# First layer of a two-layer trunk step on one core: eight mixing units multiplied from the unnormalised input

## What is computed

```python
def _rms(x, g):
    xf = x.astype(jnp.float32)
    y = xf * lax.rsqrt(jnp.mean(xf * xf, axis=-1, keepdims=True) + EPS)
    return (y * g.astype(jnp.float32)).astype(x.dtype)

def _layer(x, cond, p, lam_init, pos, ctx):
    mod = jnp.einsum('bd,de->be', jax.nn.silu(cond), p['w_ada']) + p['b_ada']
    sh1, sc1, g1, sh2, sc2, g2 = jnp.split(mod[:, None, :], 6, axis=-1)
    h = _rms(x, p['g_norm1']) * (1 + sc1) + sh1
    u = h @ p['w_in']
    gates, xa, qkv_da, xc, mla_in = jnp.split(u, IN_SPLITS, axis=-1)
    ...
```

## Time and profile before

| | |
|---|---|
| median of 3 runs | 1224.08 us (1223.28 to 1226.67) |
| the profiled execution, its time | 1223.51 us |
| its span | 1221.7 us |
| PE busy | 1208.0 us (99%) |
| DVE busy | 901.4 us (74%) |
| ACT busy | 575.6 us (47%) |
| POOL busy | 136.8 us (11%) |

### The profile page before, as it was taken

The page is one execution under the profiler, slowest core; times in us unless marked ns, Lnnn a source line. Parts: engine busy times, 40 slices in busy tenths (PEclk is TensorE's granted clock), DMA queues, the critical chain, the costliest instruction groups (busy, mean ns, idle before and its releaser), DMA issues.

```text
span 1221.7 us, 19781 instructions
## 1 busy us (share of the span) xinstructions
PE 1208.0 (99%) x7816; PEld 1149.7 (94%) x7816; DVE 901.4 (74%) x1671; ACT 575.6 (47%) x949; POOL 136.8 (11%) x109
## 2 busy tenths in 40 slices
PE   8999999999999999999999999999999999999998
PEld 7987999989989999999989889999998999999998
DVE  5597877748689999986876965765686887887432
ACT  3445564643365544532354455645425554454321
POOL 0232000008300000000202500000271000000000
PEclk9999999999999999999999999999999999999999
DMA  9763433444744444469664522332345334334443
GB/s 370 291 220 125 147 117 112 172 139 161 253 173 144 167 156 159 169 216 322 214 234 163 189 87 87 104 104 87 104 167 196 122 124 135 122 123 136 134 142 121
DMA packets 53532, 198.82 MB, mean 163 GB/s; under 512 B 6784, under 2 KB 7200, under 8 KB 51904
## 3 DMA queue, kind: packets, MB, share of 16 engines
q1 hardware_dynamic: 53120, 196.86, 46.0%
q0 software_dynamic: 320, 0.69, 0.2%
HBM read 195.25 MB, written 2.27 MB: 162 GB/s over the span
## 4 chain that ended last, share of the span: by engine, by line
PE 93%; DVE 2%; POOL 2%; DMA 1%; issue 1%; ACT 0%; SPq 0%; DVEq 0%; POOLq 0%; ACTq 0%
PE bank L1444 27%; PE bank L1446 27%; PE bank L1445 26%; PE bank L1743 1%; PE bank L1723 1%; PE bank L1512 1%; DVE w_lo L980 1%; DMA start_ada<-start_ada 1%; PE bank L1517 1%; PE bank L1516 1%; POOL wide L653 1%; PE bank L1713 1%; POOL merge_sum L655 1%; PE bank L1501 1%; PE bank L1698 1%
## 5 line engine op out<-in xcount | busy, mean ns | idle before, releaser
L1444 PE MATMUL bank<-act_hi,w_hi 128*128 128x384 f32 x1368 | 465.0, 340 | 0.7 <-DVE act_lo L1055 0.3
L1446 PE MATMUL bank<-act_hi,w_lo 128*128 128x384 f32 x1368 | 457.8, 335 | 0.0
L1445 PE MATMUL bank<-act_lo,w_hi 128*128 128x384 f32 x1336 | 446.6, 334 | 0.0
L980 DVE TENSOR_TENSOR w_lo<-w_raw,w_hi 128x1024 fp32r<-128x1024 f32 x251 | 318.9, 1272 | 114.6 <-ACT w_hi L662 113.6
L662 ACT ACTIVATE w_hi<-w_raw 128x1024 fp32r<-128x1024 f32 x251 | 264.3, 1054 | 167.8 <-DMA w_raw<-stream 167.7
L1444 PEld LDWEIGHTS bank<-act_hi,w_hi 128*128 128x128 f32 x1368 | 257.1, 188 | 10.7 <-issue 6.5
L1446 PEld LDWEIGHTS bank<-act_hi,w_lo 128*128 128x128 f32 x1368 | 256.8, 188 | 0.0
L1445 PEld LDWEIGHTS bank<-act_lo,w_hi 128*128 128x128 f32 x1336 | 251.0, 188 | 0.6
L1446 PE MATMUL bank<-mlp_hi,w_lo 128*128 128x384 f32 x352 | 118.3, 336 | 0.0
L1444 PE MATMUL bank<-mlp_hi,w_hi 128*128 128x384 f32 x352 | 118.3, 336 | 0.0
L1445 PE MATMUL bank<-mlp_lo,w_hi 128*128 128x384 f32 x352 | 118.3, 336 | 0.0
(11 more groups left out here) (246 smaller groups left out, 1576.0 us busy)
## 6 DMA issues: line engine op xcount, KB each, us to landing
w_raw<-stream SPq DMA_DIRECT2D x251, 512.0 KB, 3.3
ada<-ada_rows SPq DMA_DIRECT2D x48, 512.0 KB, 4.4
start_ada<-start_ada SPq DMA_DIRECT2D x8, 1024.0 KB, 17.9
ada_norm<-ada_w SPq DMA_DIRECT2D x16, 512.0 KB, 5.8
ada<-ada_w SPq DMA_DIRECT2D x8, 512.0 KB, 5.5
start_raw<-start_w SPq DMA_DIRECT2D x8, 448.0 KB, 18.5
ada_head_a<-ada_w SPq DMA_DIRECT2D x5, 512.0 KB, 7.3
cond_spread_mix<-cond_rows SPq DMA_DIRECT2D x2, 1024.0 KB, 7.9
```

What stands on the lines that cost most here:

```text
L980: V.tensor_tensor(wlo[s][:, :], raw[s][:, :], whi[s][:, :].bitcast(F32), ALU.subtract).then_inc(lo_ready, 1)
L1444: T.matmul(out, wb[s][0][:, w, :], hi[k], start=first and k == 0, stop=False)
L1445: T.matmul(out, wb[s][0][:, w, :], lo[k], start=False, stop=False)
L1446: ins = T.matmul(out, wb[s][1][:, w, :], hi[k], start=False, stop=last and k == n - 1)
```

## The change

- PE multiplies eight units (START_UNITS = 8) with x times scale, which is not divided by the root of the square sum, and with two more columns, the shift itself (`start_width` = 386 columns). The high and low parts of these operands are `suhi` and `sulo`. Afterwards DVE (`start_rescale`) multiplies each bank by `rstd` and ACT (`start_add_shift`) adds the product of weights and shift.
- The normalised input (`ahi`, `alo`), needed from `values` on, is still made: ACT leaves x times scale in `late` (`gated_late`), POOL multiplies it by `rstd`, ACT and DVE split it (`normed_high`, `normed_low`), by the table START_NORMED in blocks 4 to 7.
- The square sums: ACT squares two blocks at a time, POOL adds the eight squares to one block, and PE sums the partitions with one matmul in block 3, between the high and the low products.
- x is loaded in four parts, each ahead of a block's weights; START_ADA is 3, WARM 6.
- In `MIX`, `xc0` and `xc1` now stand before `k0` and `k1`, in both layers.

```diff
-START_ADA = 6
-WARM = 11
+START_ADA = 3
+WARM = 6
+START_UNITS = SKIP + 1
+START_NORMED = {4: (0,), 5: (1, 2), 6: (3, 4), 7: (5, 6)}
...
-MIX = ["xa0", "xa1", "q0", "q1", "k0", "k1", "xc0", "xc1", "v0", "v1", "cq", "ckv", "cqr"]
+MIX = ["xa0", "xa1", "q0", "q1", "xc0", "xc1", "k0", "k1", "v0", "v1", "cq", "ckv", "cqr"]
...
# SP
-            for h in range(2):
-                c0, c1 = h * KD // 2 * TOK, (h + 1) * KD // 2 * TOK
-                sp.dma_start(x_t[:, c0:c1], x_in[:, c0:c1]).then_inc(x_loaded[h], 16)
             for j in range(KD):
+                if j < KD // 2:
+                    c0, c1 = 2 * j * TOK, (2 * j + 2) * TOK
+                    sp.dma_start(x_t[:, c0:c1], x_in[:, c0:c1]).then_inc(x_loaded[j], 16)
                 if j >= START_ADA:
                     sp.wait_ge(ada_done, 2 * (j - START_ADA + 1))
...
# POOL
+                if l == 0:
+                    for h in range(KD // 2):
+                        pool.wait_ge(start_sq, h + 1)
+                        own(nc.gpsimd.tensor_tensor(wide[:, 2 * h, :], wide[:, 2 * h, :], wide[:, 2 * h + 1, :], ALU.add))
+                        own.wait()
+                        if h >= 1:
+                            own(nc.gpsimd.tensor_tensor(wide[:, 0, :], wide[:, 0, :], wide[:, 2 * h, :], ALU.add))
+                            own.wait()
+                    nc.gpsimd.sem_inc(start_sq_sum, 1)
+                    pool.wait_ge(rstd_ready, 1)
+                    for k in range(KD):
+                        pool.wait_ge(start_full, k + 1)
+                        nc.gpsimd.tensor_tensor(wide[:, k, :], late[:, k, :], rsn, ALU.mult).then_inc(norm_full, 1)
...
# ACT
+                def start_unnormed_high(j):
+                    act.wait_ge(start_shift, j + 1)
+                    for a, e, c in RANGES:
+                        ins = A(late[:, j, a:e], x[:, j, a:e], ACT.Copy, scale=sc1[:, j, c:c + 1])
+                    ins.then_inc(start_full, 1)
+                    A(suhi[:, j, TOK:start_width], mod[:, j, :], ACT.Copy)
+                    act.wait_ge(start_full, j + 1)
+                    A(suhi[:, j, 0:TOK], late[:, j, :], ACT.Copy).then_inc(start_u_hi, 1)
+                def start_add_shift(q):
+                    out = pj[:, PJ[MIX[q]], :]
+                    act.wait_ge(start_rescaled, q + 1)
+                    for a, e, c in RANGES:
+                        ins = A(out[:, a:e], out[:, a:e], ACT.Identity, bias=start_sums[:, q, c:c + 1])
+                    ins.then_inc(mix_out, 1)
                 if l == 0:
+                    for j in range(KD):
+                        if j < KD // 2:
+                            start_square(j)
+                        start_high(j)
+                        if j == KD // 2:
+                            roots(0)
+                        start_unnormed_high(j)
+                        for k in START_NORMED.get(j, ()):
+                            normed_high(0, k)
+                    split(SKIP)
+                    normed_high(0, KD - 1)
+                    split(SKIP + 1)
+                    for q in range(START_UNITS):
+                        start_add_shift(q)
+                        if q == 2:
+                            split(SKIP + 2)
+                        if MIX[q] in SQUARED:
+                            mix_squares(q)
...
# DVE
+                    start_low(j)
+                    dve.wait_ge(start_u_hi, j + 1)
+                    low(sulo[:, j, 0:TOK], late[:, j, :], suhi[:, j, 0:TOK])
+                    low(sulo[:, j, TOK:start_width], mod[:, j, :], suhi[:, j, TOK:start_width]).then_inc(start_u_lo, 1)
+                def start_rescale(q):
                     dve.wait_ge(rstd_ready, 1)
+                    dve.wait_ge(unit_done, FROM + q + 1)
+                    V.tensor_copy(start_sums[:, q, :], bank[q][:, TOK:start_width])
+                    V.tensor_tensor(pj[:, PJ[MIX[q]], :], bank[q][:, 0:TOK], rsn, ALU.mult).then_inc(start_rescaled, 1)
...
# PE
+                    pe.wait_ge(start_read, KD // 2 + 1)
+                    pe.wait_ge(start_sq_sum, 1)
+                    T.matmul(bank[7][:, P:P + TOK], cc("ones"), wide[:, 0, :], start=True, stop=True).then_inc(ss_done, 1)
...
                     pe.wait_ge(cond_ready, 1)
                     start_modulate(0)
-                    start_modulate(1)
                     for j in range(KD):
-                        start_products(j)
-                        if j + 2 < KD:
-                            start_modulate(j + 2)
+                        if 1 <= j < KD - 1:
+                            start_modulate(j + 1)
+                        start_high_products(j)
+                        if j == 0:
+                            start_modulate(1)
+                        if j == KD // 2 - 1:
+                            start_squares()
+                        start_low_products(j)
+                    unit_ready(SKIP)
+                    pe.wait_ge(mod_read, FROM + 2)
+                    dense(bank[7][:, 0:start_width], SKIP, range(KD), [suhi[:, k, :] for k in range(KD)],
+                          [sulo[:, k, :] for k in range(KD)]).then_inc(unit_done, 1)
```

More of the change, by code:

```diff
@@ L679, in square @@
                 A(wide[:, k:k + n, :], x[:, k:k + n, :], ACT.Square).then_inc(sq_ready, 1)
-            for h in range(2):
-                act.wait_ge(x_loaded[h], 16)
-                A(wide[:, 4 * h:4 * h + 2, :], x[:, 4 * h:4 * h + 2, :], ACT.Square).then_inc(start_sq_act, 1)
             own = Links(act, act_own)
@@ L708, in rstds, with roots, normed_high, norm @@
                             after[i]()
[L710 to L712 removed]
+                def roots(n):
                     act.wait_ge(ss_done, l * 2 + n + 1)
[L714 removed]
+                    sums = bank[SUM_BANK[n]][:, 0:TOK] if l + n else bank[7][:, P:P + TOK]
+                    own(A(rsn, sums, ACT.Ln, scale=1.0 / D, bias=EPSC))
                     own.wait()
                     A(rsn, rsn, ACT.Exp, scale=-0.5).then_inc(rstd_ready, 1)
[L717 removed]
+                def normed_high(n, k):
+                    shift = mod[:, 0:8, :] if n == 0 else mod[:, 24:32, :]
+                    act.wait_ge(norm_full, (l * 2 + n) * KD + k + 1)
+                    for a, e, c in RANGES:
+                        ins = A(ahi[:, k, a:e], wide[:, k, a:e], ACT.Identity, bias=shift[:, k, c:c + 1])
+                    ins.then_inc(norm_hi, 1)
+                def norm(n):
+                    roots(n)
+                    if n == 0:
                         act.wait_ge(shift_ready, l)
                     for k in range(KD):
[L720 to L726 removed]
+                        normed_high(n, k)
+                def mix_squares(u):
+                    i, rows = SQUARED.index(MIX[u]), NOPE if MIX[u] == "cqr" else P
+                    act.wait_ge(mix_out, l * U_MIX + u + 1)
+                    A(wide[0:rows, i, :], pj[0:rows, PJ[MIX[u]], :], ACT.Square).then_inc(psq, 1)
                 def start_high(j):
@@ L756, in _ @@
                     if name in SQUARED:
-                        i, rows = SQUARED.index(name), NOPE if name == "cqr" else P
-                        act.wait_ge(mix_out, l * U_MIX + u + 1)
-                        A(wide[0:rows, i, :], pj[0:rows, PJ[name], :], ACT.Square).then_inc(psq, 1)
+                        mix_squares(u)
                 def gate(g):
@@ L1038, in scales, with normed_low @@
                                                pc(gain).unsqueeze(2).to_broadcast([P, KD, 2]), ALU.add, ALU.mult))
+                def normed_low(n, k):
+                    shift = mod[:, 24 * n:24 * n + KD, :]
+                    dve.wait_ge(norm_hi, (l * 2 + n) * KD + k + 1)
+                    if l + n == 0:
+                        dve.wait_ge(start_u_lo, k + 1)
+                    for a, b, c in RANGES:
+                        ins = V.scalar_tensor_tensor(alo[:, k, a:b], wide[:, k, a:b], shift[:, k, c:c + 1],
+                                                     ahi[:, k, a:b].bitcast(F32), ALU.add, ALU.subtract)
+                    ins.then_inc(norm_lo, 1)
                 def norm(n):
-                    scale, shift = (sc1, mod[:, 0:8, :]) if n == 0 else (sc2, mod[:, 24:32, :])
+                    scale = (sc1, sc2)[n]
                     own.wait()
@@ L1098, in _ @@
                     for j in range(KD):
-                        start_norm(j)
-                    for u in range(SKIP, SKIP + 3):
-                        split(u)
+                        start_unnormed_low(j)
+                        for k in START_NORMED.get(j, ()):
+                            normed_low(0, k)
+                    split(SKIP)
+                    normed_low(0, KD - 1)
+                    split(SKIP + 1)
+                    for q in range(START_UNITS):
+                        start_rescale(q)
+                        if q == 2:
+                            split(SKIP + 2)
                 else:
@@ L1551, in values @@
                                 ins.then_inc(unit_done, 1)
```

(2 more changed lines are left out.)

126 lines of the change are left out of this document (52 added, 74 removed).

## The result

The changed kernel takes 1235.56 us (median of 4 runs, 1235.47 to 1237.72), the kernel before 1224.15 beside it: ratio 1.0099, interval 1.0085 to 1.0113. It is 11.4 us slower, where 3.35 were forecast, and outside the range of 1221.5 to 1229.5. The span grows by 12.0, from 1221.7 to 1233.7 us.

What follows compares the result with a forecast made beforehand. PE was taken as never idle from 19.77 us on, the start-up before it as bound by bytes. Terms -0.5 + 0.75 + 1.9 + 1.2 = +3.35 on 1223.51 gave 1226.8 us, range 1221.5 to 1229.5.

Steps and rivals of the forecast that it cites:

- Behind 100 us I see nothing: Rest of the kernel after 100 us: nothing gained or lost there; layer 1's new order only moves the same work.
- Term 3: Queue on ACT and DVE ahead of `values`: it starts 1.8 us after unit 7 ends; +1.9 in all, bounds 0 and 3.
- Term 1: Start of the kernel: fewer bytes of x ahead, modulation 2 at 19.25 instead of 19.77 us, -0.5 us.
- Term 2: Square sums: one f32 matmul comes back in block 3, on a PE without idle time, +0.75 us.
- blocks 4 to 7: Moved operations on ACT and DVE fit under each block's 4.87 us, costed at nothing; cover about 1 us per block.
- late bound: Start-up: PE's clock becomes high only at 17.9 us, which would make the start +0.45 us instead of -0.5.
- two extra columns: Unnormalised products: 2 columns in 384 over 192 matmuls of 0.17 us, 0.2 us, taken as inside the rounding.
- rival D: POOL stretches DVE's low parts in blocks 4 and 5; PE waits some 2.5 us, 1229.3 us; chance 0.23.
- Term 4: Row products on DVE start 4.6 us later, PE waits ahead of the products with `cq`: +1.2 us, bounds 0 and 3.3.
- B: Start: the clock is high early and bytes bound the start, -0.95 there, 1226.4 us in all; chance 0.18.
- C: Start: loads land earlier, clock high, modulation 2 at 16.8, -3.0 there; 1224.4 us, or 1221.3 without both waits; chance 0.17.

Runs made afterwards that it cites:

- filled_wait: Changed kernel with 13 small matmuls of `ones` by `ones` in PE's wait ahead of `values`: 1233.04 us, ratio 1.0079.
- shifts_first: both_fixes, with ACT doing the eight shifts in one go, then unit 10's high part, then the four squares: 1226.61 us, ratio 1.0024.
- warm_start: Changed kernel with 11 pairs of warm-up matmuls instead of 6 and 10 more matmuls behind modulation 0: 1234.07 us, ratio 1.008.
- no_shift_of_tiles: Changed kernel with its 64-byte tile `start_sums_shift` behind `start_unnormed_lo` instead of ahead of `mlp_hi`: 1231.01 us, ratio 1.0056.
- pool_held: Changed kernel with POOL's window operations held until DVE has made unit 9's low part: 1233.46 us, ratio 1.008.
- unit9_first: Changed kernel with unit 9's high part ahead of ACT's eight shifts and its low part behind DVE's first rescaling: 1231.3 us, ratio 1.0057.
- both_fixes: Changed kernel with the edits of unit9_first and no_shift_of_tiles together: 1227.4 us, ratio 1.0027.
- all_fixes: shifts_first with 11 pairs of warm-up matmuls and 10 more matmuls behind modulation 0: 1226.53 us, ratio 1.0025.
- mlp_tiles_64_on_before: Kernel before with `mlp_hi` and the tiles laid behind it 64 bytes further on, no instruction changed: 1226.76 us, ratio 1.002.
- x_behind: all_fixes with most of x loaded behind the modulation weights 2 and 3, and ACT's squares behind the unnormalised parts: 1229.35 us, ratio 1.0039.

## Why the prediction was wrong

Two steps failed. The sentence "Behind 100 us I see nothing that takes it back or adds to it" put the new tile, which shifts all tiles behind it, at nothing, and there 4.8 us were lost, 4.6 of them on matmul steps by the count above. And Term 3, the wait ahead of `values`, was sized 1.8 us and priced at its length; it was 3.25, with 1.55 more at half clock behind it. Up to 97.77 us the lag of 7.2 is 0.62 (Term 1), 0.65 (Term 2), 0.44 (blocks 4 to 7), 0.5 (386 columns) and 5.0 (Term 3, counted from start to start).

**Term 1 (-0.5) was +0.62.** The steps in it hold: modulation 0 at 8.72 (8.3), products 0 at 12.97 (12.8), half clock in both. I took 16 us for the rise of the clock and had 17.9 as the late bound; records fall from 0.69 to 0.34 us between 17.35 and 18.36, so in this execution the late bound was it. The size of this term is an accident of the execution: seven kernels share the instructions of this start, and in their profiled executions modulation 2 comes at 19.24 (filled_wait), 19.34, 20.07, 20.19, 20.39, 20.50 and 21.10 (shifts_first). The forecast's 19.25 is at the early end of them. That bytes bound the rest at 18.7 to 18.8 is shown by warm_start. The Trainium skill (TensorE: Matmul & The Clock Gate, Part 1: The HAM clock gate) says that the throttled state is the default; the trace agrees, with a first modulation of 1.94 us that takes 1.10 later.

**Term 2 (+0.75) was +0.65** (the block that holds L1562 takes 5.55 us, from 30.23 to 35.78, and the two ahead of it 4.94 and 4.90). Right. The two extra columns were not "inside the rounding": 0.2 was said, but a step with 386 columns takes 177.4 ns in unit 7 (4.08 us over 23 steps, 54.69 to 58.77) against 173.5 before. On 192 records that is 0.75 us, some 0.5 of it behind modulation 2. It is 177.4 in no_shift_of_tiles too, which does not clear the address: there the start of `start_unnormed_hi` moves from remainder 0 by 256 to 192, but that of `start_unnormed_lo` from 64 to 0. The cause is open.

**Blocks 4 to 7 (0) were +0.44**, by rival D's mechanism: POOL's five multiplications in a row beside DVE's low part.

```profile
34.64 5.27 POOL L618 TENSOR_TENSOR wide<-gated_late,rstd 128x384 f32<-128x384 f32 x5 [7.54 <-ACT rstd L688]
```
```profile
35.85 1.20 DVE L1047 TENSOR_TENSOR start_unnormed_lo<-gated_late,start_unnormed_hi 128x384 fp32r<-128x384 f32 x1 [2.80 <-ACT start_unnormed_hi L688]
36.97 0.97 DVE L1047 TENSOR_TENSOR start_unnormed_lo<-mod,start_unnormed_hi 128x2 fp32r<-128x2 f32 x1
37.86 2.33 DVE L1111 SCALAR_TENSOR_TENSOR act_lo<-wide,mod,act_hi 128x128 fp32r<-128x128 f32 x2
```

2.33 us for a pair that takes 0.74 when POOL is idle. I had priced D at 2.5 there; it was 0.44 there and 1.0 at `values`, where I had not looked. DVE is the one that is held, and pool_held gives it back. The Trainium skill (GPSIMD Engine Reference, 1. Specifications) says that GpSimd shares its SBUF interfaces with VectorE and contends with VectorE instructions that have two SBUF inputs. The rows agree: L1111 reads `wide` and `act_hi`, and takes 3.1 times as long.

**Term 3 (+1.9) was +4.8.** The place, the releaser and the cause were right, unit9_first shows them. The wait was sized 1.8 and is 3.25: 1.0 by POOL, the rest because ACT's shifts start at 56.64, 2.3 us ahead of the end of unit 7 and not 3.0 (54.0 against 57.0). And I costed a wait at its length. PE came back at half its clock for 3.3 us, 1.55 us more; filled_wait gives 1.47 of it back.

**Term 4 (+1.2) was 0 in the changed kernel**, and not because it was wrong: the row products start at 69.92, 7.22 later than at 62.70, and PE is 7.21 later too. The larger Term 3 covered it. As soon as Term 3 is repaired it is there, with 0.6 to 1.1 us (unit9_first, both_fixes, all_fixes).

**"Behind 100 us I see nothing" was the largest error:** +4.8 us. The diff shows a tile inserted ahead of `top`; I read it as storage and not as an address of every tile behind it. mlp_tiles_64_on_before shows the effect for `mlp` without the change, no_shift_of_tiles for all three. The count of steps, 4.6, leaves 0.2 us of the span's 12.0, but as a balance: PE waits 0.5 us more for `ada` weights here, a wait that varies from 0.7 to 1.8 between executions, and 0.7 less for DVE's `w_lo` at `merged` (2.94 against 3.63 us in four waits), probably because PE arrives there later. Some 0.4 us stay unexplained.

**Rivals.** B and C: warm_start makes C's clock high and still gets 18.70; its 16.8 needs x out of the way (x_behind, 16.84), which the change does not do. D was true in part.

## What to carry to other kernels

Treat a tile inserted ahead of others as a change of address of them all, and compare the step of a long gapless matmul stretch before and after. Here it was enough to put the new tile behind the others. Cost a wait on PE at its length and, beside it, at what a spell at half clock behind it may add (here 1.2 to 1.55 us, where it came), and put the low part that PE waits for ahead of work whose reader is later. Before you count on a gain at the start, work out what the next bound allows: here bytes allowed 1 us, and a repaired chain each time handed the time to the next.
